# Where the operands of TensorE begin in SBUF: transposed x and turned attention output moved to 64 bytes past a multiple of 128

## What is computed

```
for l in range(2):                                   # first block
    proj = x @ w_in[l]                               # gated linear attention + sparse attention
    mix  = concat(hgrn2(...), nsa(...)) @ w_out[l]
    x    = layer_norm(ALPHA * x + mix)
    ffn  = (silu(x @ w_gate[l]) * (x @ w_up[l])) @ w_down[l]
    x    = layer_norm(ALPHA * x + ffn)
for l in range(2):                                   # second block
    proj = rms_norm(x) @ w_in_2[l]                   # MLA, differential and window attention
    x    = x + (sum_b sigmoid(gate_b) * (o_b @ w_branch[b])) @ w_out_2[l]
    h    = rms_norm(x)
    x    = x + (gelu(conv(h @ w_gate_2)) * (h @ w_up_2)) @ w_down_2
    x    = x + sigmoid(rms_norm(x) @ w_ple_gate) * rms_norm(pe @ w_ple_proj)
```

## Time and profile before

| | |
|---|---|
| median of 3 runs | 1728.37 us |
| profiled execution, its own time | 1727.11 us |
| its span (first to last instruction) | 1725.3 us |
| TensorE matmul busy | 1653.6 us (96%) |
| TensorE weight load busy | 1504.2 us (87%) |
| VectorE, ScalarE, GpSimd busy | 68%, 53%, 26% |
| mean granted TensorE clock | 0.986 |
| DMA, mean over the span | 167 GB/s |

### The profile page before, as it was taken

How to read it: one execution, slowest core, us unless ns; L and a number is a source line. 1 busy time by engine, 2 the same in 40 slices (tenths; PEclk the granted TensorE clock), 3 DMA queues, 4 the chain that set the end, 5 groups by cost and what they waited for, 6 DMA issues and landing times.

```text
span 1725.3 us, 30143 instructions
## 1 busy us (share of the span) xinstructions
PE 1653.6 (96%) x11354; PEld 1504.2 (87%) x11354; DVE 1170.4 (68%) x1601; ACT 921.4 (53%) x1576; POOL 441.4 (26%) x184
## 2 busy tenths in 40 slices
PE   8989999999988999999999999999999999999997
PEld 6878799989887899978899989999788999899996
DVE  5687754467786545476884877666767856777677
ACT  5664554446645544465655564545755555554445
POOL 2212122212121322224511132222235211222222
PEclk9999999999999999999999999999999999999999
DMA  9432455646523665546333455655554333466653
GB/s 332 157 119 96 161 199 185 201 147 210 162 78 122 220 193 188 191 153 213 113 110 100 140 199 184 215 185 182 180 194 146 110 100 116 161 218 199 207 183 127
DMA packets 82563, 288.74 MB, mean 167 GB/s; under 512 B 9051, under 2 KB 11908, under 8 KB 81924
## 3 DMA queue, kind: packets, MB, share of 16 engines
q1 hardware_dynamic: 77352, 272.58, 48.1%
q10 hardware_dynamic: 5084, 14.37, 2.5%
HBM read 284.81 MB, written 2.11 MB: 166 GB/s over the span
## 4 chain that ended last, share of the span: by engine, by line
PE 62%; DVE 7%; ACT 3%; issue 2%; DVEq 0%; ACTq 0%
PE bank L720 30%; PE bank L737 25%; PE bank L1294 2%; DVE w_lo L686 2%; PE bank L1275 1%; PE bank L1266 1%; ACT w_hi L682 1%; PE bank L765 1%; PE bank L1254 1%; PE bank L1307 0%; DVE qk L2528 0%; PE bank L1186 0%; PE bank L774 0%; PE bank L910 0%; DVE z L2502 0%
## 5 line engine op out<-in xcount | busy, mean ns | idle before, releaser
L686 POOL TENSOR_TENSOR w_lo<-raw,w_hi 128x1024 fp32r<-128x1024 f32 x146 | 375.3, 2570 | 1175.7 <-ACT w_hi L682 1175.7
L686 DVE TENSOR_TENSOR w_lo<-raw,w_hi 128x1024 fp32r<-128x1024 f32 x364 | 558.2, 1558 | 153.9 <-ACT w_hi L682 151.5
L682 ACT ACTIVATE w_hi<-raw 128x1024 fp32r<-128x1024 f32 x510 | 520.0, 1052 | 101.6 <-PE bank L737 46.3
L720 PE MATMUL bank<-x_t_hi,w_hi 128*128 128x256 f32 x1984 | 321.4, 284 | 5.3 <-ACT gl L1430 2.9
L720 PE MATMUL bank<-x_t_hi,w_lo 128*128 128x256 f32 x1984 | 313.9, 280 | 0.0
L720 PE MATMUL bank<-x_t_lo,w_hi 128*128 128x256 f32 x1984 | 313.5, 280 | 0.0
L720 PEld LDWEIGHTS bank<-x_t_hi,w_hi 128*128 128x128 f32 x1984 | 273.9, 190 | 16.8 <-issue 5.1
L720 PEld LDWEIGHTS bank<-x_t_hi,w_lo 128*128 128x128 f32 x1984 | 268.7, 189 | 0.0
L720 PEld LDWEIGHTS bank<-x_t_lo,w_hi 128*128 128x128 f32 x1984 | 268.2, 189 | 0.0
L737 PE MATMUL bank<-w_hi,x_t_hi 128*128 128x512 f32 (+3 forms) x448 | 136.1, 387 | 9.4 <-issue 5.8
L737 PE MATMUL bank<-w_hi,x_t_lo 128*128 128x512 f32 (+3 forms) x448 | 133.5, 381 | 1.5 <-DVE x_t_lo L1962 1.5
(11 more groups left out here) (390 smaller groups left out, 2128.0 us busy)
## 6 DMA issues: line engine op xcount, KB each, us to landing
raw<-stream SPq DMA_DIRECT2D x511, 512.0 KB, 4.3
rows<-rows ACTq DMA_DIRECT2D x4, 1024.0 KB, 4.6
gain<-rows ACTq DMA_DIRECT2D x8, 512.0 KB, 4.6
hv_p<-hv_dram ACTq DMA_DIRECT2D x14, 256.0 KB
x<-x_in SPq DMA_DIRECT2D x2, 512.0 KB, 5.0
bias_r<-rev_dram SPq DMA_DIRECT2D x1, 1024.0 KB, 7.3
hv_dram<-hv ACTq DMA_DIRECT2D x2, 512.0 KB, 7.4
y_out<-x SPq DMA_DIRECT2D x2, 512.0 KB, 2.7
```

Source lines behind the costliest of these rows:

```text
L682: self.eng.activation(w_hi[:, i, :], raw[:, i, :], ACT.Copy).then_inc(hi_done.sem, 1)
L686: self.eng.tensor_tensor(w_lo[:, i, :], raw[:, i, :], w_hi[:, i, :].bitcast(F32), ALU.subtract).then_inc((lo_pool if self.part == "pool" e ...
L720: mm = pe.matmul(target, a[:, i, w0 + kt * P:w0 + (kt + 1) * P], b[:, k0 + kt, :], start=kt + k == 0, stop=k == 2 and kt == kts - 1)
```

## The change

It moves tiles in SBUF and changes nothing else: each engine has the same instructions in the same order, with the same waits.

```diff
-        top = [nc.sbuf_base + (-nc.sbuf_base) % 64]
-
-        def sb(name, shape, dtype=F32, at=None):
+        top = [nc.sbuf_base + (-nc.sbuf_base) % 32]
+
+        def sb(name, shape, dtype=F32, at=None, line=None):
 
             size = 4 * int(np.prod(shape[1:]))
+            if line is not None:
+                top[0] += (line - top[0]) % 128
             if at is None:
                 at = top[0]
-                top[0] += size + (-size) % 64
+                top[0] += size + (-size) % 32
...
-        raw = sb("raw", [P, RING, UNIT])
+        raw = sb("raw", [P, RING, UNIT], line=0)
...
-        top[0] += 32
-        x_t_hi = sb("x_t_hi", [P, KT, S], F32R)
+        x_t_hi = sb("x_t_hi", [P, KT, S], F32R, line=64)
         x_t_lo = sb("x_t_lo", [P, KT, S], F32R)
-        top[0] += 32
...
-        o_base = top[0]
-        o_t_hi = sb("o_t_hi", [P, 12, S], F32R)
+        o_t_hi = sb("o_t_hi", [P, 12, S], F32R, line=64)
+        o_base = top[0] - 12 * S * 4
...
-        arena = top[0]
-        param1 = sb("param1", [P, N_PARAM1])
+        param1 = sb("param1", [P, N_PARAM1 + -N_PARAM1 % 32], line=0)
         rows_at = top[0]
+        arena = rows_at - 4 * (N_PARAM1 + -N_PARAM1 % 32)
...
-        top[0] += 4 * (N_PARAM1 + -N_PARAM1 % 8)
+        top[0] += 4 * (N_PARAM1 + -N_PARAM1 % 32)
...
-                act.dma_start(param1[:], param1_in[at.reg]).then_inc(params_loaded.sem, 16)
+                act.dma_start(param1[:, 0:N_PARAM1], param1_in[at.reg]).then_inc(params_loaded.sem, 16)
```

## The result

| | before | after |
|---|---|---|
| median of 8 runs each, in turn | 1728.38 us (1725.13 to 1729.87) | 1733.29 us (1731.13 to 1735.15) |
| ratio after/before | | 1.0031, 95% interval 1.0020 to 1.0042 |
| profiled execution, its own time | 1727.11 us | 1733.15 us |
| its span | 1725.3 us | 1731.4 us |
| mean granted TensorE clock | 0.986 | 0.987 |

The account below looks back on a forecast made before the run. TensorE, busy 96% of the span, bounds the kernel by products times pace. Terms -12.5, -4.2, -2.5 and -0.4 sum to -19.6 us, times 0.85 is -16.7: 1711.7 us beside the median, range 1692 to 1739.

Parts of the forecast that it names:

- Step 1: x_t streamed, distance 32 to 64, 5952 products: pace falls from 116.7 to 114.6 ns, -12.5 us (bounds -46 to +18).
- Step 2: x_t held, 512 columns streamed, 1056 products: pace falls to 229 ns, -4.2 us (between -6.6 and +6.6).
- Step 3: o_t streamed, distance 0 to 64, 576 products: from 119 to 114.6 ns, -2.5 us.
- Step 4: o_t held, 96 products: from 233 to 229 ns, -0.4 us.
- the marker: The 12 hs products in 2.75 us stay as they are; if they move too, distance is the wrong idea.
- Step 5: VectorE, ScalarE and GpSimd on moved tiles: at most 7 to 13 ns ride on an offset; taken as 0.
- step 6: DMAs: the same columns are sent, and a faster TensorE gets the 2% more it asks for; 0.
- Step 7: Who keeps up: VectorE and ScalarE have room to split weights faster, but softmax and normalisation chains don't shrink; factor 0.85.
- the factor 0.85: Share of TensorE's gain on its own path that reaches the end: 62 of 74 points of the chain of waits.
- rival A: The period is 64 bytes, so x_t at 64 streams as at 0: +10.4 us, 1739 us, slower; chance 0.19.
- B: Distance is not the cause, or 64 streams like 32: 1723 with the held gain (0.13), 1728 with nothing (0.09).
- C: At 64 the reads don't meet, streamed products take 109 ns: -50 us, 1679; 0.11 including what lies toward the forecast.

Follow-up runs that it names:

- e3: The changed kernel with x_t back at 32 bytes (consts kept at 64), o_t still at 64: 1726.76 us, ratio 0.9990.
- e6: The kernel before with x_t_hi and x_t_lo at 64 bytes and no other tile moved: 1735.64 us, ratio 1.0043.
- e2: The grid of e1 with ScalarE, VectorE and DMA kept busy beside TensorE: paces within 0.3 ns a product of the quiet grid, but for the first group.
- e13: The changed kernel with both parts of x_t 112 from the weights modulo 256, o_t at 192, hs at 0: 1716.51 us, ratio 0.9950.
- e12: The changed kernel with x_t and o_t 192 from the weights modulo 256, hs at 0: 1721.99 us, ratio 0.9974.
- e4: The changed kernel with x_t at 0 and consts kept at 64: 1737.93 us, ratio 1.0056.
- e1: The first grid: no model, TensorE alone, groups of 48 products at varied operand beginnings; 113.3 to 123.4 ns for 256 columns, 226.7 to 234.6 for 512.
- e11: The loop and its table: no model, feed-forward products plus 24 with x held, x at 0 to 240 and beyond; 48 streamed took 5.45 to 5.76 us.
- e5: No model: 28 products at a fixed position after 12 others, with or without a short product between; at distance 192, 113.3 or 117.8 ns.

## Why the prediction was wrong, point by point

**What bounds the kernel: right.** The time followed TensorE's pace both ways, and all of the loss shows: +4.7 us busy, +4.9 us in the median, +6.1 in the span of the profiled executions.

**Step 1, x_t streamed from 32 to 64, is the step that failed.** It took "the step already seen once more" and put 114.6 ns where 116.7 had been. The measured pace, start to start inside its runs, is 117.6 on average against 116.8. Added up from start to start over the whole execution, with the waits left out, TensorE spends 713.0 us on these products where it spent 709.8: +3.2 us instead of -12.5. (0.7 x 5952 would be +4.3; the changed kernel had 12 fewer intervals of over 150 ns.) The mistake has two parts that the runs separate. First, two points made a slope, and there is none: the table goes 5.75, 5.70, 5.60, 5.69, 5.66, 5.75, 5.76, 5.48. Second, the point for distance 0 was o_t, which is at 128 in the modulus that counts. That did little harm here, since 0 and 128 stream nearly alike (5.75, 5.76). The bounds held the result; the choice between them had no ground.

**Step 2, x_t held: 0 instead of -4.2.** 233.3 ns before and 233.4 after. The end "as 32 did, 0" was right. The step reached for the 227 of hs as something that 64 should at least equal, but 227 belongs to distances 0, 16, 144 and 240. Its range is also written as "-6 x 1056 = -6.6", which is 6.3 x 1056. Of the 288 narrower products that the step left out, the 96 with 256 columns went from 118.2 to 113.5 ns, or -0.4 us, and the others moved by 0.3 us or less.

**Step 3, o_t streamed: -0.1 us instead of -2.5.** Inside its runs it came to 117.8 ns, the pace of x_t at the same distance, from 118.6. The rule "same distance, same pace" held, with its size wrong with step 1. But 288 products take 34.40 us where they took 34.47, because each run has one more interval, of some 213 ns; where that comes from is not known. **Step 4**: 96 products from 233 to 233, as step 2.

**What no step had: the runs of hs.** A run of 12, counted to the start of the next product, went from 2.744 to 2.757 us without having moved; for 88 such runs that is +1.1 us. The prediction said that in this case distance is the wrong idea. e3 puts them back to 2.744 by moving only x_t, so the idea stands and the marker was badly chosen: an unmoved run can change because the run ahead of it hands over differently. The starts show where the time goes. Before, the products of a run follow each other after 230, 236, 228, 233 and 231 ns, then 226.7 on average; in the changed kernel and in e6 after 241, 224, 231, 236, 228, 233 and 231 ns, then the same 226.7. The steady pace is untouched, and the run takes two products longer to reach it. What is handed over is not seen in any run. Counted as in step 1, the parts are x_t streamed +3.2, hs +0.9, x_t held +0.5 and o_t streamed -0.1: +4.5 of the +4.7 us that TensorE is busier.

**Step 5 and step 6: right.** L1962 and L1419, in the form of the earlier trace rows:

```profile
L1962 DVE TENSOR_TENSOR x_t_lo<-bank,x_t_hi x40: 678/684/692, 9.0 to 1706.5; 128x512 fp32r<-128x512 f32 x40
...
L1419 ACT ACTIVATE x_t_hi<-bank x40: 579/597/601, 7.7 to 1705.8; 128x512 fp32r<-128x512 f32 x40
```

4 ns and 0 ns off. e2 shows as much for DMA: at 388 GB/s the products keep their pace.

**Step 7, the factor 0.85, was not needed.** Lost time passed through whole, as rival A had said of it. As for gains, the two that were made disagree: e13 passed all of its 10.8 us on (span 1713.7, 11.6 less), e12 with the same busy time only 3.7. The rest of e12 went into waits of TensorE. Its span less its busy time is 78.8 us, where before it is 71.7 and in e13 70.9, and no single kind of wait grew by more than 1.5 us; the largest is for VectorE's `merged_b` ahead of the branch products. e13 has that wait too and still stays at 70.9; why is open.

**The rivals.** A gave the right sign by the wrong mechanism. It wanted 64 to equal 0: e4 has 0 at 119.9 ns and 1737.93 us, and a period of 64 is refuted. Its own deciding point (streamed above 117.3, nothing gained held) was met all the same. That the stated range holds the measured time is owed to the room it left for A, and is luck as far as the forecast's mechanism goes. B's first half, traffic, is refuted by e2; its second, that 64 streams like 32, missed by 0.7 ns a product, which is most of the loss. C, no meeting at all, never came near: no place of 256 columns was faster than 113.3 ns in any run.

The Trainium skill's rule was weighed in the prediction: "SBUF — State Buffer", section "Who interferes with whom", with independent read ports and a TensorE that waits on no one. By it the change was worth nothing. Toward the other engines the runs agree with it (e2, within 0.3 ns). Between TensorE's own two reads they are against it: 113.3 to 123.4 ns for the same form of product, with only the addresses changed and all other engines idle (e1). It came closer to the time than the forecast did, by 5 us against 22, without being true. The formula that the prediction took from the Trainium skill, "TensorE: Matmul & The Clock Gate", section "Back-to-back issue gap", is given there for an isolated product and not for a stream with a load for each, so the trace's distance from it decides nothing.

**What stays open.** Why certain distances cost, and what state a run leaves to the next, is not shown. That the two operands' relative position modulo 256 changes the pace is shown (e1, e3, e4, e6, e11, e13); the picture of two reads that meet in the memory is only a picture. What picks the slow rhythm at 192 is known only as "what runs ahead" (e5), and at 64 not even that is shown. Steering the entry inside the kernel wasn't tried. The first grid and the loop also disagree at some distances, as at 112 (120.0 with the held tile at 16, against 5.48/48 = 114.2 ns), 144 (118.7 against 116.7) and 208 (116.7 against 119.2). At 208 the entry is a cause: e5 has the grid's own products there at 119.2 to 119.4. So a pace belongs to a loop and its entry and not to a distance alone.

## What to carry to other kernels

When an engine is busy 96% of the time, its pace per instruction deserves a look at addresses, but two positions in a trace don't make a slope: run the kernel's own inner loop over the full period, with its real steps and with every part of an operand (high and low) in place, and trust the table only if it gives back the rows of the kernel that exists. Read paces from start to start or from the chain's counts. After a change of placement also look at the runs that did not move, for they can be entered in another rhythm.

## What the hardware showed that was not expected

- The relative position of the held and the streamed operand changes the pace of a 256-column fp32r product between 113.3 and 123.4 ns and that of a 512-column one between 226.7 and 234.6 (e1). In the loop the paces repeat after 256 bytes and not after 128 (e11). Full DMA, VectorE and ScalarE load changed it by no more than 0.3 ns outside the first group (e2).
- At distance 192 the same products at the same addresses run at 113.3 or at 117.8 ns, chosen by the products ahead and, after five intervals or fewer, kept to the end of the run (e5). The changed kernel shows both at 64.
- A run whose operands did not move can still lose: the hs runs need two products more to reach the same 226.7 ns when x_t ahead of them moves from 32 to 64 (2.744 to 2.757 us).
- The best place for streaming is not the best for holding: 112 streams 48 products in 5.48 us and holds 24 in 5.60; 0 streams in 5.75 and holds in 5.44 (e11).
